# A two-block mixed model on one core: RWKV's key length by logarithm and exponential, and waits for GpSimd's powers as steps of the weave

## The reference, cut to what matters

```python
kk = hs(k * k_k)
kk = kk / jnp.maximum(jnp.sqrt(jnp.sum(kk * kk, axis=-1, keepdims=True)), 1e-12)
```

```python
var = jnp.mean(jnp.square(y - mean), axis=-1, keepdims=True)
y = ((y - mean) * lax.rsqrt(var + RWKV_LN_EPS)).reshape(b, s, -1) * ln_w + ln_b
```

## Time and profile before

| | us |
|---|---|
| median of three executions | 3916.73 |
| span of the profiled execution, first to last instruction | 3913.3 |
| what the median is above that span | 3.4 |
| TensorE busy with matmuls | 3798.5 (97%) |
| VectorE busy | 2256.0 (58%) |
| ScalarE busy | 1795.6 (46%) |
| mean granted TensorE clock | 0.985 of full speed |

### The profile page before, as it was taken

The page is one execution under the profiler, slowest core; times in us unless marked ns, Lnnn a source line. Parts: engine busy times, 40 slices in busy tenths (PEclk is TensorE's granted clock), DMA queues, the critical chain, the costliest instruction groups (busy, mean ns, idle before and its releaser), DMA issues.

```text
span 3913.3 us, 49190 instructions
## 1 busy us (share of the span) xinstructions
PE 3798.5 (97%) x19948; PEld 3204.6 (82%) x19948; DVE 2256.0 (58%) x3532; ACT 1795.6 (46%) x2519; POOL 104.5 (3%) x61
## 2 busy tenths in 40 slices
PE   8999999999999999989999999999999989999998
PEld 7886778787898897778888888988987778888887
DVE  5665666675555746764454444566656664445444
ACT  6454545445454424544444444545325454444443
POOL 0000000000010000000000000010000000000000
PEclk9999999999999999999999999999999999999999
DMA  7655546563554405446666655544225446666654
GB/s 239 184 167 147 145 135 179 158 188 101 182 165 135 122 26 159 146 146 190 191 188 189 200 194 193 178 125 143 63 78 153 152 140 189 192 189 189 201 193 169
DMA packets 341426, 628.34 MB, mean 161 GB/s; under 512 B 21088, under 2 KB 63024, under 8 KB 340432
## 3 DMA queue, kind: packets, MB, share of 16 engines
q1 hardware_dynamic: 331920, 611.53, 51.7%
q10 hardware_dynamic: 9280, 13.69, 1.1%
HBM read 623.04 MB, written 2.10 MB: 160 GB/s over the span
## 4 chain that ended last, share of the span: by engine, by line
PE 88%; DVE 6%; ACT 3%; POOL 1%; issue 1%; DMA 1%; SPq 0%; ACTq 0%; DVEq 0%; POOLq 0%
PE bank L621 74%; DVE weights_low L527 2%; PE bank L745 1%; PE bank L1320 1%; PE bank L1417 1%; PE bank L2524 1%; PE bank L2538 1%; PE bank L2131 1%; PE bank L2537 1%; ACT weights_high L514 1%; PE bank L600 1%; PE bank L1400 1%; POOL stat L706 0%; PE bank L1323 0%; POOL arena L706 0%
## 5 line engine op out<-in xcount | busy, mean ns | idle before, releaser
L527 DVE TENSOR_TENSOR weights_low<-weights,weights_high 128x1024 fp32r<-128x1024 f32 (+3 forms) x1176 | 1393.7, 1195 | 979.0 <-ACT weights_high L514 967.7
L514 ACT ACTIVATE weights_high<-weights 128x1024 fp32r<-128x1024 f32 (+3 forms) x1176 | 1206.9, 1030 | 1341.2 <-PE bank L621 1284.1
L621 PE MATMUL bank<-weights_high,x_high 128*128 128x512 f32 (+3 forms) x2816 | 1116.7, 397 | 21.4 <-DVE weights_low L527 9.7
L621 PE MATMUL bank<-weights_low,x_high 128*128 128x512 f32 (+3 forms) x2816 | 1086.3, 386 | 0.0
L621 PE MATMUL bank<-weights_high,x_low 128*128 128x512 f32 (+3 forms) x2816 | 1086.0, 386 | 0.0
L621 PEld LDWEIGHTS bank<-weights_high,x_high 128*128 128x128 f32 x2816 | 536.0, 190 | 135.4 <-DVE weights_low L527 17.2
L621 PEld LDWEIGHTS bank<-weights_low,x_high 128*128 128x128 f32 x2816 | 535.0, 190 | 101.8
L621 PEld LDWEIGHTS bank<-weights_high,x_low 128*128 128x128 f32 x2816 | 536.3, 190 | 93.1
L621 PE MATMUL bank<-x_high,weights_high 128*128 128x256 f32 x960 | 279.6, 291 | 12.2 <-DVE arena L650 6.0
L621 PE MATMUL bank<-weights_high,y_high 128*128 128x512 f32 (+1 forms) x672 | 266.2, 396 | 8.7 <-DVE weights_low L527 6.5
L621 PE MATMUL bank<-weights_high,ff_high 128*128 128x512 f32 x704 | 274.0, 389 | 0.0
(11 more groups left out here) (385 smaller groups left out, 3618.8 us busy)
## 6 DMA issues: line engine op xcount, KB each, us to landing
weights<-in_w_in_dram SPq DMA_DIRECT2D x208, 512.0 KB, 3.6
weights<-in_w_ffn_gate_dram SPq DMA_DIRECT2D x176, 512.0 KB, 3.7
weights<-in_w_ffn_up_dram SPq DMA_DIRECT2D x176, 512.0 KB, 3.6
weights<-in_w_ffn_down_dram SPq DMA_DIRECT2D x176, 512.0 KB, 3.6
weights<-in_w_out_dram SPq DMA_DIRECT2D x128, 512.0 KB, 3.6
weights<-in_even_w_in_dram SPq DMA_DIRECT2D x88, 512.0 KB, 3.6
weights<-in_odd_w_in_dram SPq DMA_DIRECT2D x80, 512.0 KB, 3.6
weights<-in_mem_w_kv_dram SPq DMA_DIRECT2D x32, 512.0 KB, 4.2
```

The costliest lines, as they stand in the source:

```text
L514: self.high_mark[g] = self.high_split.count(act.ran(nc.scalar.activation(high, raw, ACT.Copy)), act.clock)
L527: self.low_mark[g] = self.low_split.count(dve.ran(nc.vector.tensor_tensor(low, raw, high.bitcast(F32), ALU.subtract)), dve.clock)
L621: ins = pe.ran(nc.tensor.matmul(out, l, r, start=(u + c + x + y == 0), stop=(u == blk.n - 1 and c == UNIT - 1 and y == 1)))
```

## The change

`inv_rms` is split: `power_begun` does the scaling on VectorE and the power on GpSimd and returns the power's mark; `inv_rms` is that and the wait. In `prep`, in `head_rms_gate` and at the end of `rwkv` the task now begins the power, yields its mark, and only then lets VectorE wait. The 14 other uses are as before. In `rwkv` the root and the reciprocal are replaced: VectorE takes max(sum, 1e-24) out of PSUM as each matmul is done, ScalarE takes Ln of the whole tile and Exp of -0.5 times that, and the task yields Exp's mark before VectorE waits for it.

```diff
-    def inv_rms(self, ss, n, eps=EPS):
+    def power_begun(self, ss, n, eps=EPS):
         pool.wait_ge(dve.did(nc.vector.tensor_scalar(ss, ss, 1.0 / n, eps, ALU.mult, ALU.add)))
-        mark = pool.did(nc.gpsimd.tensor_tensor(ss, ss, self.minus_half[0:ss.shape[0], 0:ss.shape[1]], ALU.pow))
-        dve.wait_ge(mark)
+        return pool.did(nc.gpsimd.tensor_tensor(ss, ss, self.minus_half[0:ss.shape[0], 0:ss.shape[1]], ALU.pow))
+
+    def inv_rms(self, ss, n, eps=EPS):
+        mark = self.power_begun(ss, n, eps)
+        self.dve.wait_ge(mark)
         return mark
@@ prep
-            for k in range(0, at, 32):
-                self.inv_rms(stats[:, k:min(at, k + 32)], 1)
+            powers = [self.power_begun(stats[:, k:min(at, k + 32)], 1) for k in range(0, at, 32)]
+            yield powers
+            dve.wait_ge(*powers)
@@ head_rms_gate
-        self.inv_rms(ss, HD2)
+        power = self.power_begun(ss, HD2)
+        yield [power]
+        dve.wait_ge(power)
@@ rwkv, the key's length
-            act.wait_ge(pe.did(pe.ran(nc.tensor.matmul(self.ps[6 + g][:, :], self.c("pair_ones"), sq[:, g * 512:(g + 1) * 512], start=True, stop=True))))
-        for g in range(2):
-            m = act.did(nc.scalar.activation(sq[:, g * 512:(g + 1) * 512], self.ps[6 + g][:, :], ACT.Sqrt))
+            pe.did(pe.ran(nc.tensor.matmul(self.ps[6 + g][:, :], self.c("pair_ones"), sq[:, g * 512:(g + 1) * 512], start=True, stop=True)))
+            dve.wait_ge(pe.now())
+            m = dve.did(nc.vector.tensor_scalar(sq[:, g * 512:(g + 1) * 512], self.ps[6 + g][:, :], 1e-24, None, ALU.max))
             self.bank_free[6 + g] = [m]
+        act.wait_ge(m)
+        act.seq(nc.scalar.activation(sq, sq, ACT.Ln))
+        m = act.did(nc.scalar.activation(sq, sq, ACT.Exp, scale=-0.5))
...
+        yield [m]
         dve.wait_ge(m)
-        dve.seq(nc.vector.tensor_scalar(sq, sq, 1e-12, None, ALU.max))
-        dve.seq(nc.vector.reciprocal(sq, sq))
-        yield
@@ rwkv, the last normalisation
-        self.inv_rms(st, HD2, LN_EPS)
+        power = self.power_begun(st, HD2, LN_EPS)
         dve.did(nc.vector.tensor_tensor(tmp, v3, bonus.rearrange("p t h -> p (t h)").unsqueeze(2).broadcast_to([P, T * H2, HD2]), ALU.mult))
+        yield [power]
+        dve.wait_ge(power)
```

## The result

The changed kernel took 3869.01 us (median of four executions, 3862.2 to 3880.25) against 3914.52 us; ratio 0.9889, 95% interval 0.9876 to 0.9901. It is 45 us faster, where I had forecast 16 and a range down to 3886. Run again with the later experiments it took 3871.38 us (3868.72 to 3876.13, five executions) against 3913.66, ratio 0.9898 (0.988 to 0.9916).

The account below looks back on a forecast made before the run. TensorE was taken as the bound, only its standing or lower clock winnable; 11.2 (reciprocal) + 2.5 (prep) + 2.4 (rwkv's end) + 0 (head_rms_gate) = 16.1 us, giving a median of 3901 us, range 3886 to 3920.

Parts of the forecast that it names:

- sign of being wrong: Prediction is wrong if TensorE's idle time falls by more than 15 us, or the share of low clock grows.
- What bounds the kernel: TensorE, busy 3798.5 of 3913.3 us; only its standing or lower clock can be won, where weights_low came late.
- The reciprocal: In rwkv, both layers: waits of 1.7 and 3.4 us and 6.1 us of clock go; 11.2 us, bounds 3.4 to 11.2.
- prep's powers: Eight places in prep: weights_low goes ahead of the scaling at three; 2.5 us, or 3.3 with free overlap.
- the three places: In prep, powers with TensorE waits of 1.6, 0.6 and 1.1 us right behind; priced 1.2 + 0.6 + 0.7 us.
- the five: prep's other five powers: no TensorE wait behind them, so they give nothing.
- The end of rwkv: Power at rwkv's end in both layers: one 1.23 us instruction leaves the way, 1.2 + 1.2 = 2.4 us; bounds 2.4 and 7.7.
- my value: VectorE's work stands until GpSimd's power is done; layer 0's 4.7 us wait at rwkv's end becomes 3.5.
- head_rms_gate: Six places, a chain of power, scaling and product at layer 1's retention; 0 us, bounds -5 and +5.
- open question of the overlap: How soon weights_low runs beside a GpSimd power; taken to stand until it ends, as beside HGRN's subtraction.
- free overlap: Rival: nothing stands beside a power and all terms take their upper ends; 27.2 us, 3889.5; chance 0.15.
- The other rivals: Clock stays low, 3911, 0.25; stream spent too early, 3926, 0.12; change doesn't do what it says, 3905, 0.03.

Follow-up runs that it names:

- The reciprocal in four: Kernel before with the reciprocal cut into four of 128x256, a yield after each; ratio 1.0014, 3918.4 us.
- the key alone: Kernel before with only the key's length by Ln and Exp instead of root and reciprocal, powers as before; ratio 0.9958, 3896.1 us.
- the gate alone: Kernel before with only head_rms_gate's 6 powers yielded before VectorE's wait; ratio 0.9981, 3907.5 us.
- the reciprocal told short: Kernel before with the planner told 1.2 us instead of 6.6 us for a reciprocal, same instructions; ratio 0.9983, 3908.2 us.
- lead 5 on the changed kernel: Changed kernel with VectorE's allowed lead 5.0 instead of 3.0 us before a stream piece is put in front; ratio 0.9938 to the kernel before, 3892.3 us.
- all powers together: Kernel before with the powers at all 16 places yielded before VectorE's wait, root and reciprocal as before; ratio 0.9927, 3885.5 us.
- the three parts: Kernel before with powers yielded only in prep (8), only in head_rms_gate (6), or only at RWKV's end (2); ratios 0.9972, 0.9981, 0.9988.

## Why the prediction was wrong

The prediction's own sign of being wrong came true: TensorE's idle time fell by 29.2 us, where it allowed 15. Its sum had 10.0 us of waits and 6.1 of clock; the measured gain of 42 to 45 has some 27 to 29 and 15.

**What bounds the kernel**: right that only TensorE's standing and clock count. Wrong in the next sentence, that what counts is where a `weights_low` came late because VectorE stood, read from the waits right behind each power. TensorE takes a fixed amount of work per layer; if a task's chain is late by some us, the weave fills TensorE with stream pieces at that point, and no wait need show there. It shows elsewhere: at the layer's end, where the pieces are spent, or in another lane's attention 40 us on. The reciprocal in four shows that the local waits aren't the price: both gone, the time no better.

**The reciprocal**: 11.2 us forecast, 16.4 measured alone, though not in the places that I had booked. The waits of 1.7 and 3.4 us are gone in the changed kernel, and 2724 to 2738 has the clock at 1.00:

```profile
2724.00:2738.00 14.00, 14.00 (x115) 14.00 (x115) 13.50 (x26) 8.39 (x10) 0.00 (x0) 1.00 0.37 103
```

Details were off in small: in layer 1 ScalarE had waited 2.1 us for the `pair_ones` matmul and not about 1.2; each floor took 0.69, my upper end, not 0.5; from the second floor's end (1299.7) to Exp's (1303.2) it was 3.5 us, not 4.7, since Ln's table load was out of the way before. With the key alone, layer 1's RWKV is 5.7 us shorter (first row, against 255.1), where 9.5 were booked, and layer 0 gave nothing in its profiled execution, where 1.7 were. The larger part is at the layer's end, which the forecast didn't have at all: the last two mixers are 10.8 us shorter, and TensorE's idle time in them fell from 18.0 to 9.6 us:

```profile
2703.90:2953.30 249.40, 244.41 (x1603) 219.51 (x1602) 154.62 (x260) 91.43 (x142) 8.71 (x3) 0.95 0.31 89
2953.30:3148.40 195.10, 185.49 (x904) 148.94 (x902) 131.62 (x313) 97.72 (x163) 6.46 (x3) 1.00 0.48 154
```

**prep's powers**: the largest miss, 2.5 forecast and 11 measured. The step that failed is the pricing of the three places by their own waits (0.6 and 0.7 us for the two wide ones): these two give 8.6 us, and the one at 405 us stands beside another lane's attention. The other six places give the rest, 2.4 us or nothing within the intervals, so "give nothing" may stand for the five. That they have "no TensorE wait behind them" was misread. Behind the power at 943.71 us of the kernel before stands the longest of all of TensorE's waits:

```profile
PE bank L745 <- DVE arena L1148: 7.8, 1, 7.8
```

The power (1.65 us) and four scalings (2.51 us) lie one behind the other in its chain, and it is 7.8 us in the changed kernel too (until 938.7 us).

**The end of rwkv**: 2.4 forecast, 4.7 (1 to 8) measured, inside my bounds. I took the end of the bounds where VectorE stands for the power; the trace shows the other: the 4.7 us wait is 1.0 us in the changed kernel, where my value said 3.5 and the other end 1.4.

**head_rms_gate**: 0 forecast, 7.4 (4 to 11) measured, above my bound of 5, though its interval reaches below it. The sentence that fails is that the 5.8 us wait at layer 1's retention "can't shrink by more than one 1.2 us instruction". With the gate alone, and the same 117 matmuls left, it is 2.2 us shorter:

```profile
PE bank L749 <- DVE arena L1956: 3.6, 1, 3.6
```

Where the rest of the 7.4 us comes from, no run parts. In the changed kernel the wait for line 1950's product (1957 now) is gone. That is not the gate's doing: 180 matmuls are left there, and in the runs with the key alone and with the reciprocal told short, which have 180 left too and the gate as before, it is gone as well. What is left in the changed kernel is 1.5 us for another reason:

```profile
PE bank L749 <- DVE arena L682: 1.5, 1, 1.5
```

**The open question of the overlap**: my value was wrong, and the rival "free overlap" named the right mechanism, with 27 us a price still too low by 15 to 18, as it too summed local waits. My value rested on the subtraction's row, and no row of a power beside VectorE's work was there to hold against it. The Trainium skill's rule of the shared port ("SBUF — State Buffer", at the diagram's reading) says the loser stands for the other's whole instruction. In this trace that holds for HGRN's subtraction and not for a power: four `weights_low` ran at full speed in 3.25 us beside it. What can be seen of the rule is the 0.9 us by which the power is longer when a 128x1024 VectorE instruction with two inputs in SBUF is under way as it begins.

The other rivals did not come: the clock in layer 1 did not stay low, and the stream was spent later, not earlier (180 left instead of 117). That one looked at the right quantity, with the wrong sign. Its premise about the clock, that only stream pieces keep it up in RWKV, doesn't fit the trace of the kernel before. Here are the stream's matmuls (line 621) alone in two windows; 2860 to 2880 has none, 176 others, and the clock at 1.00:

```profile
2860.00:2880.00 20.00, 0.00 (x0) 0.00 (x0) 1.00 0.01 2
2900.00:2917.00 17.00, 9.70 (x33) 8.57 (x32) 0.51 0.32 97
```

No wait of TensorE stands before the second window either (the last ends at 2751), so the lower clock doesn't only follow the longer gaps, as the prediction's first paragraph has it. This stretch is gone in the changed kernel's profiled execution, and the forecast booked nothing for it; what brings it on is open.

What stays open: why versions that leave still more of the stream for the end lose (lead 5 on the changed kernel, 20 us), since its layers' lengths changed in several places at once; how the key's gain divides between VectorE's real time and the planner's order; why the gate gives 7.4 us; and the rest of about 5 us between all powers together and the three parts.

## What to carry to other kernels

Where a planner fills one engine's gaps with work from a second list, the waits right behind a slow instruction are not its price: compute how far it pushes the tasks' chain against that list, and look at the stretch where the list runs out. A blocking wait on one lane's tiny operation stops every lane that shares the queue, so put the wait behind a yield, and do so first at the longest operation (two 5.4 us powers gave 8.6 us). To part an engine's real time from the order that a planner makes of it, change the told cost and the real cost separately, and compare only runs in which the planner left the same amount of the second list.

## What the runs showed of the hardware

GpSimd's power of 128x16 or 128x32 (2.90 and 5.43 us) didn't hold up VectorE's two-input instructions in SBUF (1.22 us of `weights_low` beside the power at 404.23), while its 128x1024 subtraction did (a `weights_low` of 2.92 us instead of 1.22 at the longest, the second of the earlier trace rows). ScalarE loaded a table for Exp right behind Ln (1.28 us each, lines 2399 and 2400), and for Ln right behind Exp. The same program's mean granted clock differs between executions, and its time with it: over 23 executions of the kernel before it was 0.981 to 0.988, and the times span 17.4 us; nine executions of the changed kernel, in two sessions, span 18 us (3862.2 to 3880.25).
